# Layer norms on VectorE, their first four feature tiles turned first and used for two units; queries from unscaled input, turned twice

## What is computed

```python
# first block, after each of its two layers
x = _layer_norm(DEEPNORM_ALPHA * x + y, ln_g[layer], ln_b[layer])
# start of the second layer of the first block
q_lat, gate = hproj[..., :Q_LORA], hproj[..., Q_LORA:]     # hproj = x @ w_in
c = x @ w_down
# second block
h = rms_norm(x, norm1_w)
u = h @ w_in        # rnn_x, rnn_gate, q, k, v, iq, ik, iw, g
```

## Time and profile before

| | us |
|---|---|
| median of 3 runs | 933.73 |
| lowest, highest | 932.53, 934.49 |
| the profiled execution | 932.19 |
| its span | 930.8 |
| PE, DVE, ACT, POOL busy | 916.8, 582.2, 496.6, 91.5 |
| first norm: last warm-up start to first product | 204.85 to 214.86 |
| second norm: the same | 476.90 to 492.66 |

### The profile page before, as it was taken

The page is one execution under the profiler, slowest core; times in us unless marked ns, Lnnn a source line. Parts: engine busy times, 40 slices in busy tenths (PEclk is TensorE's granted clock), DMA queues, the critical chain, the costliest instruction groups (busy, mean ns, idle before and its releaser), DMA issues.

```text
span 930.8 us, 14040 instructions
## 1 busy us (share of the span) xinstructions
PE 916.8 (98%) x5964; PEld 838.1 (90%) x5964; DVE 582.2 (63%) x769; ACT 496.6 (53%) x616; POOL 91.5 (10%) x68
## 2 busy tenths in 40 slices
PE   9999999998999999999989999999999999999998
PEld 8798897888899999998868899999999899998887
DVE  5866576467866666665475758768567655554441
ACT  6445444335766666664336467786763465554330
POOL 0010110010001111111020000121200012220000
PEclk9999999999999999999998999999999999999999
DMA  9834455533453334356544525433254645556530
GB/s 355 325 135 176 163 206 197 176 113 128 168 187 142 142 142 142 142 182 222 170 177 155 206 91 183 136 97 131 92 180 143 221 141 182 183 187 213 181 112 23
DMA packets 24830, 154.67 MB, mean 166 GB/s; under 512 B 3136, under 2 KB 3520, under 8 KB 9024
## 3 DMA queue, kind: packets, MB, share of 16 engines
q1 hardware_dynamic: 22880, 148.97, 44.8%
q10 hardware_dynamic: 1728, 4.28, 1.6%
q0 software_dynamic: 160, 0.52, 0.1%
HBM read 152.72 MB, written 1.05 MB: 165 GB/s over the span
## 4 chain that ended last, share of the span: by engine, by line
PE 87%; ACT 5%; DVE 5%; issue 2%; DMA 1%; SPq 0%; ACTq 0%; DVEq 0%
PE ps L332 26%; PE ps L334 26%; PE ps L333 26%; ACT w_hi_ring L849 1%; ACT c_p L1224 1%; PE ps L553 1%; PE ps L554 1%; PE ps L574 1%; DMA w_raw<-in_a_w_in 1%; PE ps L388 1%; PE ps L460 1%; PE ps L564 1%; PE ps L728 1%; PE ps L680 1%; DVE w_lo_ring L1265 1%
## 5 line engine op out<-in xcount | busy, mean ns | idle before, releaser
L1265 DVE TENSOR_TENSOR w_lo_ring<-w_raw,w_hi_ring 128x2048 fp32r<-128x2048 f32 x146 | 342.1, 2353 | 220.6 <-ACT w_hi_ring L849 220.3
L849 ACT ACTIVATE w_hi_ring<-w_raw 128x2048 fp32r<-128x2048 f32 x146 | 278.0, 1911 | 129.2 <-PE ps L334 123.7
L332 PE MATMUL ps<-xT_hi,w_hi_ring 128*128 128x256 f32 x776 | 222.2, 286 | 0.5 <-DVE w_lo_ring L1271 0.5
L334 PE MATMUL ps<-xT_hi,w_lo_ring 128*128 128x256 f32 x776 | 219.4, 283 | 0.0
L333 PE MATMUL ps<-xT_lo,w_hi_ring 128*128 128x256 f32 x776 | 219.4, 283 | 0.0
L332 PEld LDWEIGHTS ps<-xT_hi,w_hi_ring 128*128 128x128 f32 x776 | 148.7, 192 | 2.1 <-issue 1.3
L333 PEld LDWEIGHTS ps<-xT_lo,w_hi_ring 128*128 128x128 f32 x776 | 148.8, 192 | 0.7
L334 PEld LDWEIGHTS ps<-xT_hi,w_lo_ring 128*128 128x128 f32 x776 | 148.7, 192 | 0.0
L332 PE MATMUL ps<-w_hi_ring,xT_hi 128*128 128x512 f32 (+1 forms) x272 | 107.0, 393 | 0.2 <-DVE xT_lo L1281 0.2
L334 PE MATMUL ps<-w_hi_ring,xT_lo 128*128 128x512 f32 (+1 forms) x272 | 104.6, 384 | 0.0
L333 PE MATMUL ps<-w_lo_ring,xT_hi 128*128 128x512 f32 (+1 forms) x272 | 104.4, 384 | 0.0
(11 more groups left out here) (315 smaller groups left out, 1585.0 us busy)
## 6 DMA issues: line engine op xcount, KB each, us to landing
w_raw<-in_a_w_in SPq DMA_DIRECT2D x22, 1024.0 KB, 4.9
w_raw<-in_w_ff_in SPq DMA_DIRECT2D x16, 1024.0 KB, 4.9
w_raw<-in_w_ff_out SPq DMA_DIRECT2D x16, 1024.0 KB, 4.8
w_raw<-in_b_w_uq SPq DMA_DIRECT2D x16, 576.0 KB, 4.0
...
```

What stands on the lines that cost most here:

```text
L332: k.T.matmul(out, lh, rh, start=start, stop=False, skip_group_check=True)
L334: return k.T.matmul(out, ll, rh, start=False, stop=stop, skip_group_check=True)
L849: k.A.activation(k.hi[:, u % RING, :], k.raw[u % RING][:, :], ACT.Copy).then_inc(k.s["w_hi"], 1)
L1265: k.V.tensor_tensor(k.lo[:, u % RING, :], k.raw[u % RING][:, :], k.hi[:, u % RING, :].bitcast(F32), ALU.subtract).then_inc(k.s["w_lo"], 1)
```

## The change

- The layer norm is done by DVE for both token tiles, by halves of the features: the first 512 features of both tiles are centred and scaled first, the second half later. `act_layer_norm` and `pool_layer_norm` are gone.
- PE turns the first four feature tiles of t = 0 as they come, runs 12 products of `keep_warm`, turns those of t = 1. It uses these four tiles for the first unit, then turns the other four and goes on (`pe_turn_normed`). The order of the units of weights follows: two output groups with the first half of the features, then both with the second.
- Before the query units the turned tiles are those of the norm's result without the second root. The root is taken meanwhile (`act_squares`), and multiplied in when the sums are copied out. The scaled `c_h` is still made, beside the units, and turned after the last two of them, over `xT`, for the recurrence units ("hs").
- The index keys come before the seventh query unit instead of behind the eighth. Squares and sums by head of queries move up behind the drain of group 1 and of group 2. Those of keys stay late, in a place of their own (`c_hk`).

Of code that is replaced as a whole (the query units' loops, `act_layer_norm`) the diff shows the new lines; the old ones stand above.

```diff
-WARM = (20, 36)
+WARM = 12
...
-        load(k, U_QLAT + n, d["b_w_qlat"][n // 2, n % 2])
+        load(k, U_QLAT + n, d["b_w_qlat"][n % 2, n // 2])
...
-        load(k, U_QKVI + n, d["w_qkvi"][n // 2, n % 2])
+        load(k, U_QKVI + n, d["w_qkvi"][QKVI[n]])
...
+def pe_turn_normed(k, layer, b):
+    for t in range(NT):
+        k.T.wait_ge(k.s[f"ln_t{t}"], 2 * layer + b + 1)
+        for pair in (2 * b, 2 * b + 1):
+            for n in range(2):
+                tile = 2 * pair + n
+                m = k.T.transpose(k.ps[:, 4 + pair, (2 * n + t) * P:(2 * n + t + 1) * P], k.res[:, t, tile * P:(tile + 1) * P],
+                                  k.ident[:, :])
+            if t == NT - 1:
+                m.then_inc(k.s["turned"], 1)
+        if b == 0 and t == 0:
+            keep_warm(k, WARM)
...
-    keep_warm(k, WARM[0])
-    for n in range(4):
-        T.wait_ge(s["ln_t0"], n // 2 + 1)
-        T.wait_ge(s["ln_t1"], n // 2 + 1)
-        pe_turn_pair(k, "a", n, lambda t, c: k.res[:, t, c * P:(c + 1) * P], ps[:, 4 + n, :])
+    pe_turn_normed(k, 0, 0)
     pe_latents(k)
     for pair in range(HB // 2):
         pe_pair(k, pair)
     pe_output(k, 1, U_BOUT, k.b_oT, pe_attention_hooks(k))
-    keep_warm(k, WARM[1])
     pe_hybrid(k)
     pe_feed_forward(k)
...
-        b, half = n // 2, n % 2
+        half, b = n // 2, n % 2
+        if n == 1:
+            pe_turn_normed(k, 0, 1)
         token_major(k, U_QLAT + n, k.xT, 4 * half, 4, 384, [ps[:, 2 * b + t, 0:384] for t in range(NT)], half == 0, half == 1,
-                    ("turned_lo", TURN["a"]) if b == 0 else None)
+                    ("turned_lo", TURN["a"]))
...
+QKVI = ((0, 0), (1, 0), (0, 1), (1, 1), (2, 0), (2, 1), (3, 0), (3, 1))
+HS_BANKS = ((6, 7), (4, 5))
...
+def pe_hybrid(k):
+    T, s, ps = k.T, k.s, k.ps
+    pe_turn_normed(k, 1, 0)
+    for n, (b, half) in enumerate(QKVI):
+        if b >= 2 and half == 0:
+            T.wait_ge(s["c_drain_a"], b - 1)
+            T.wait_ge(s["c_drain_v"], b - 1)
         if n == 1:
-            T.wait_ge(s["c_ikw"], 1)
+            pe_turn_normed(k, 1, 1)
+        if n == 6:
+            pe_index_keys(k)
+        token_major(k, U_QKVI + n, k.xT, 4 * half, 4, 512, [ps[:, 2 * (b % 2) + t, :] for t in range(NT)],
+                    half == 0, half == 1, ("turned_lo", TURN["h"]) if n < 4 else None)
+        if b == 3:
+            T.wait_ge(s["c_h0"], half + 1)
+            T.wait_ge(s["c_h1"], half + 1)
+            if half == 1:
+                T.wait_ge(s["c_ikw"], 1)
+            for c in range(2):
+                pe_turn_pair(k, "hs", 2 * half + c, lambda t, c: k.c_h[:, t, c * P:(c + 1) * P], ps[:, HS_BANKS[half][c], :])
+    T.wait_ge(s["c_drain_a"], 3)
+    T.wait_ge(s["c_drain_v"], 3)
+    for n in range(4):
+        if n == 1:
+            T.wait_ge(s["c_drain_a"], 4)
+            T.wait_ge(s["c_drain_v"], 4)
             pe_to_features(k, 0, "iq", 0)
             pe_to_features(k, 1, "iq", 2)
             pe_to_features(k, 2, "q", 0)
...
-    act_layer_norm(k, 0)
-    for n in range(4):
+    for t in range(NT):
+        act_root(k, ROOT["ln0"] + t, [z[:, t:t + 1] for z in k.tmp])
+    for n in range(4):
+        if n == 2:
+            act_hi(k, U_QLAT + AHEAD - 1)
         act_turned(k, "a", n, ps[:, 4 + n, :], k.xT[0])
-    act_hi(k, U_QLAT + AHEAD - 1)
     act_latents(k)
     for pair in range(HB // 2):
         act_pair(k, pair)
     act_attention_output(k)
-    act_layer_norm(k, 1)
+    for t in range(NT):
+        act_root(k, ROOT["ln1"] + t, [z[:, t:t + 1] for z in k.tmp])
...
+def act_squares(k):
+    A, s = k.A, k.s
+    for b in range(2):
+        cols = slice(b * 512, (b + 1) * 512)
+        for t in range(NT):
+            A.wait_ge(s[f"ln_t{t}"], 2 + b + 1)
+            m = A.activation(k.c_junk[:, t, cols], k.res[:, t, cols], ACT.Square, accum_out=k.c_squares[:, b, t:t + 1])
+    m.then_inc(s["c_sq"], 1)
+    act_root(k, ROOT["rms"], k.tmp)
...
-        A.wait_ge(s["w_used"], U_QKVI + 2 * b + 2)
-        bank = ps[:, 2 * (b % 2), :]
+    act_hi(k, U_QKVI + AHEAD)
+    act_squares(k)
+    for n in range(1, 8):
+        act_hi(k, U_QKVI + n + AHEAD)
+        if n == 1:
+            A.wait_ge(s["c_total"], 1)
+            for b in range(2):
+                cols = slice(b * 512, (b + 1) * 512)
+                A.activation(k.c_h[:, 1, cols], k.res[:, 1, cols], ACT.Copy, scale=k.rs[:, 1:2]).then_inc(s["c_h1"], 1)
+        elif n == 6:
+            A.wait_ge(s["c_ikw_mm"], 1)
+            for t in range(NT):
+                m = A.activation(k.c_ikw[:, t, :], ps[:, 4 + t, 0:2 * ID + IH], ACT.Copy, scale=k.rs[:, t:t + 1])
+            m.then_inc(s["c_ikw"], 1)
+            for c in range(2):
+                act_turned(k, "hs", c, ps[:, HS_BANKS[0][c], :], k.xT[0], vec["norm1_w_2"])
+        elif n == 7:
+            for c in range(2):
+                act_turned(k, "hs", 2 + c, ps[:, HS_BANKS[1][c], :], k.xT[0], vec["norm1_w_2"])
+        b, half = QKVI[n]
+        if half == 0:
+            continue
+        A.wait_ge(s["w_used"], U_QKVI + n + 1)
...
+            A.wait_ge(s["c_drain_a"], 2)
+            A.wait_ge(s["c_drain_v"], 2)
+            for t in range(NT):
+                m = A.activation(k.c_junk[:, t, :], k.c_qk[:, t, 0:D], ACT.Square)
+            m.then_inc(s["c_sq"], 1)
...
+    def centre(t, b):
+        r = k.res[:, t, cols[b]]
+        own.mark(V.scalar_tensor_tensor(r, r, k.mv[:, t, 0:1], lnw[:, 0, cols[b]], ALU.subtract, ALU.mult))
+    def root(t):
+        col = slice(t, t + 1)
+        V.wait_ge(s["rs_std"], ROOT[f"ln{layer}"] + t + 1)
+        own.mark(V.reciprocal(rs[:, col], std[:, col]))
+        own.wait()
+        own.mark(V.tensor_scalar(std[:, col], rs[:, col], rs[:, col], var[:, col], ALU.mult, ALU.mult))
+        own.wait()
+        own.mark(V.tensor_scalar(std[:, col], std[:, col], -0.5, 1.5, ALU.mult, ALU.add))
+        own.wait()
+        own.mark(V.tensor_tensor(rs[:, col], rs[:, col], std[:, col], ALU.mult))
+    def scale(t, b):
+        r = k.res[:, t, cols[b]]
+        own.wait()
+        V.scalar_tensor_tensor(r, r, rs[:, t:t + 1], lnw[:, 1, cols[b]], ALU.mult, ALU.add).then_inc(s[f"ln_t{t}"], 1)
     add(0, 0)
     add(0, 1)
-    root(0, lambda: add(1, 0))
-    V.scalar_tensor_tensor(k.shift[:, 0:1], k.mv[:, 0, 0:1], -1.0, k.rs[:, 0:1], ALU.mult, ALU.mult).then_inc(s["ln_shift"], 1)
+    variance(0)
+    V.wait_ge(s[f"lnw{layer}_in"], 32)
+    centre(0, 0)
+    root(0)
+    add(1, 0)
+    scale(0, 0)
     add(1, 1)
-    root(1, centre)
-    for b in range(2):
-        cols = slice(b * 512, (b + 1) * 512)
-        r = k.res[:, 1, cols]
-        V.scalar_tensor_tensor(r, r, k.rs[:, 1:2], lnw[:, 1, cols], ALU.mult, ALU.add).then_inc(s["ln_t1"], 1)
+    variance(1)
+    centre(1, 0)
+    root(1)
+    scale(1, 0)
+    centre(0, 1)
+    turned(0)
+    turned(1)
+    centre(1, 1)
+    scale(0, 1)
+    scale(1, 1)
...
 def dve_hybrid(k):
     V, s, ps, own, vec = k.V, k.s, k.ps, k.v_own, k.vec
-    V.wait_ge(s["columns_in"], 16)
+    dve_lo(k, U_QKVI + AHEAD - 1)
+    for n in (2, 3):
+        dve_turned(k, "h", n, ps[:, 4 + n, :], k.xT, vec["norm1_w_2"])
+    dve_lo(k, U_QKVI + AHEAD)
     V.wait_ge(s["c_sq"], 1)
     own.mark(V.tensor_tensor(k.c_squares[:, 0, :], k.c_squares[:, 0, :], k.c_squares[:, 1, :], ALU.add))
     own.wait()
     dve_root(k, ROOT["rms"], k.c_squares[:, 0, :], k.rs[:, :], 1e-6, k.tmp, 1.0 / D)
     V.sem_inc(s["c_total"], 1)
-    for b in range(2):
-        cols = slice(b * 512, (b + 1) * 512)
-        V.wait_ge(s["ln_t0"], 2 + b + 1)
...
-def pool_layer_norm(k, layer):
...
-        cols = slice(b * 512, (b + 1) * 512)
-        r = k.res[:, 0, cols]
-        G.wait_ge(s["ln_scaled"], 2 * layer + b + 1)
-        own.mark(G.tensor_tensor(r, r, lnw[:, 0, cols], ALU.mult))
-        own.wait()
-        G.tensor_tensor(r, r, lnw[:, 1, cols], ALU.add).then_inc(s["ln_t0"], 1)
...
```

150 lines of the change are left out of this document (56 added, 94 removed).

## The result

The changed kernel takes 922.82 us (median of 4 runs, 922.10 to 923.83), the kernel before 933.60 (4 runs beside it, 932.53 to 934.49): ratio 0.9888, 95% interval 0.9877 to 0.9900. The forecast was 924.0 with a range of 921.5 to 928.5.

A forecast was written before the change was run, and what follows sets the result against it. TensorE was taken to bound the kernel, busy 98% of the span. First norm 2.85 plus second norm 6.9 gave 9.75 off the profiled 932.19, so 922.4; with 1.5 for the median, 924.0, range 921.5 to 928.5.

The forecast's parts named there:

- First norm: First layer norm: first latent unit at 211.1 for 214.86, 3.75 earlier; 2.85 net of transposes moved behind the first unit.
- Centres at 0.8, and the root: First norm on VectorE: without POOL's operations a centre takes 0.80, upper end 1.78; the root's four small operations 0.7.
- Second norm: Second layer norm: first query unit at 483.6 for 492.66, 9.05 earlier; with clock and costs, 6.9 net.
- The clock in the first unit: First query unit behind the second norm: 2.4 GHz throughout instead of half speed in part, 0.85 gained.
- What comes back: Transposes moved behind units: 0.9 given back at the first norm, 0.9 and 1.8 at the second, plus a 0.3 wait.
- The wait at the keys: Behind the sixth query unit: PE waits 0.3 for c_kw_lo, 0 at the low end, 2.65 at the high.
- The median: Whole kernel: median of runs taken 1.5 above the profiled execution, so 922.4 becomes 924.0.
- Rival 2: Both norms: the clock falls all the same, 1.7 a norm, 3.4 for both, giving 927.4; chance 0.12.
- Rivals 1, 3 and 4: Query-unit queues late, 926.4 (0.15); gain taken back in later attention, 933.7 (0.06); weight-slot ring makes it slower, 935.7 (0.05).

The follow-up runs named there:

- run 2: The changed kernel again with no edit: median 922.90 us, ratio 0.9895 to the kernel before; four executions from 922.13 to 925.34.
- Run 6: The kernel before with only the first norm changed (VectorE norm, turns, 12 warm-up products, order of latent units): 928.53 us, ratio 0.9957.
- run 8: The changed kernel with eight 128x512 products on POOL beside the first norm, feeding nothing: 924.86 us profiled, the other three 928.61 to 929.05, ratio 0.9956.
- run 5: The kernel before with 52 instead of 36 warm-up products at the second norm: 931.66 us, ratio 0.9981.
- run 7: The kernel before with the changed first norm and the second norm on VectorE alone, query path as before: 927.13 us, ratio 0.9937.

## Why the prediction was right

The sum gave 922.4 for an execution at full clock, and there the kernel takes 922.1 (the profiled one of run 2, 922.27). The profiled execution beside the prediction took 923.83, for it lost the clock at the first norm. In run 2's profiled execution the first query unit starts at 480.83 and the first unit of the recurrence at 532.46, for 480.8 and 532.6 foretold. It came out right because each path was summed operation by operation, and the operations were in the trace.

- **First norm.** From last add to first product 6.05 was foretold, 6.06 measured; first latent unit at 211.1 foretold, 210.90 in one profiled execution and 211.12 in the other. Run 6 has 3.1 net for 2.85. No step of it is off by more than 0.1: last add to centre 1.76 for 1.75, centre and root 1.55 for 1.5, scale and wake-up 0.80 for 0.90, turned and split 1.95 for 1.90.
- **Centres at 0.8, and the root.** The centres are 0.74 in all eight, just below the low end of 0.8 to 1.78. That POOL's operations had made them slow is shown by run 8, which puts such operations back and has 1.52. The forecast named the centres alone. But it took the root at 0.7, the time of four small operations elsewhere, and in the kernel before the root took 2.59 (209.23 to 211.82): two of its five small operations waited for POOL as well, and end 0.01 to 0.02 behind POOL's, the one below and the one at 210.51 in the earlier trace rows.

```profile
208.72 1.71 POOL L1845 TENSOR_TENSOR res<-res,lnw 128x512 f32<-128x512 f32 x1
...
209.41 1.03 DVE L1300 TENSOR_TENSOR norms<-norms 128x1 f32<-128x1 f32 x1
...
210.87 0.92 DVE L1306 TENSOR_TENSOR norms<-norms 128x1 f32<-128x1 f32 x1
```

The root is 0.89 now, so 1.7 of the 3.75 comes from it: the sum had that gain without saying where it came from. The Trainium skill, "SBUF — State Buffer", "Who interferes with whom", says that the two share a port under a lock and that the loser blocks fully, and these rows and run 8 agree.

- **Second norm.** 6.5 from last add to first product foretold, 6.54 measured, where the kernel before has 15.56 (477.10 to 492.66): 9.0 gained for 9.05. The clock in the first unit gives 0.7 for 0.85 (5.55 for 6.25, run 2; 5.53 in run 5). Of the 9.0, run 7 has 1.4 from the norm and 0.7 from transposes at full clock; the rest is the order. The half speed of the kernel before began earlier than the 489.4 of the forecast, while PE was idle: its clock is 0.83 from 486 to 488 and 0.50 from 488 on.
- **What comes back.** Each group of eight transposes costs 0.79 from its first to the next product (487.70 to 488.49), where I took 0.9. The wait at the keys is nothing where I took 0.3, the low end that I had given: counted from the first query unit, c_kw_lo is over after 33.2 us for 33.8 foretold, and PE is there after 33.7 for 33.5. From the first query unit to the first of the recurrence it is 51.65 (482.13 to 533.78): 49.64 before, plus 3.0 and less 0.85 gives 51.8 foretold.
- **The median.** The one term that was mis-sized: 1.5 on top of the profile's sum, which I took over from the kernel before as spread. It is no spread but the clock: in about half of all executions of either kernel it falls once more, by the profiles of the result and of run 5 at the first norm. The kernel before was profiled without it and its median has it; the changed kernel's median has half of it, 922.8, not 924.0. That the measured median still lies well inside the range is owed to the width of the range, not to this term.
- **Rival 2** (0.12) took place in part, at the first norm, and my ground against it was poor: "the clock stayed at 1.00" at the first norm was one execution of the kernel before. Run 5 shows a fall at that same place with that same code. The price I gave, 1.7 for a norm and 3.4 for both, is 1.4 and 3.1 in run 2. Four of eight executions fell, one of them (0.996) presumably at both norms. The second norm, which by the mean clock fell in nearly every execution before, is what the change cures: 4.14 us idle became 0.60 and 1.77. Why it then falls less often than the first norm, whose waits are shorter (0.62 and 1.29), no run shows.
- **Rivals 1, 3 and 4** fell: no wait for c_kw_lo or for w_lo in the query units, and what the norms gave arrived at the end.

One thing that I did not weigh and that decided nothing: on the changed kernel the first norm's gap is shorter than before and falls no less often (four in eight against 15 in 32; of these falls one has a profile).
